# RWKV-7 scan: the second half of a triangular inverse on four 64x64 tiles of TensorE, its odd blocks swapped by VectorE transposes, with other queue orders

## The reference, cut to what matters

```python
def step(s, inp):
    r_t, w_t, k_t, v_t, a_t, b_t = inp
    sa = jnp.einsum('bhij,bhj->bhi', s, a_t)
    s = s * w_t[:, :, None, :] + sa[..., None] * b_t[:, :, None, :] + v_t[..., None] * k_t[:, :, None, :]
    return s, jnp.einsum('bhij,bhj->bhi', s, r_t)
```

## Time and profile before

| | us |
|---|---|
| median of 3 runs | 2571.04 (2567.44 to 2571.35) |
| the profiled execution, its own time | 2572.18 |
| span of the profile, first to last instruction | 2570.4 |
| stretch of the scan | 937 (1440 to 2377 us of the span) |
| one period of the scan, typical | 11.80 |
| TensorE / VectorE / ScalarE / GpSimd busy over the span | 2311.9 / 1137.1 / 798.5 / 622.8 |

### The profile page before, as it was taken

One profiled execution on the slowest core, in us unless ns is written; L12 is line 12 of the kernel. 1 busy time (PEld: TensorE's weight loads), 2 busy tenths in 40 slices (PEclk: granted clock), 3 DMA queues, 4 the chain that ended last, 5 costly groups with the idle time before them and its releaser, 6 DMA issues. The chain is left out here.

```text
span 2570.4 us, 56958 instructions
## 1 busy us (share of the span) xinstructions
PE 2311.9 (90%) x24172; PEld 1455.2 (57%) x24172; DVE 1137.1 (44%) x2231; ACT 798.5 (31%) x2003; POOL 622.8 (24%) x913
## 2 busy tenths in 40 slices
PE   5799999989969998999999598989898998988598
PEld 2355555544534443554444477777777777777354
DVE  3111111111354667002131466666666666666684
ACT  2100111102323553221000244444444444444221
POOL 0000000001221332000000444444445454544242
PEclk8899999999979998999999799999999999999699
DMA  6500000033011665555431334333333333231532
GB/s 257 212 25 16 16 16 16 16 149 129 27 41 30 176 192 157 161 154 175 163 114 58 104 92 149 92 85 94 84 94 83 92 83 93 83 95 50 186 122 87
DMA packets 296657, 261.79 MB, mean 102 GB/s; under 512 B 105440, under 2 KB 255200, under 8 KB 293856
## 3 DMA queue, kind: packets, MB, share of 16 engines
q1 hardware_dynamic: 296416, 258.32, 32.2%
HBM read 178.54 MB, written 79.69 MB: 100 GB/s over the span
## 5 line engine op out<-in xcount | busy, mean ns | idle before, releaser
L770 PE MATMUL ps<-xt,w_slab 128*128 128x512 f32 (+1 forms) x1376 | 552.7, 558 | 30.3 <-DMA w_slab<-in_w 19.5
L770 PEld LDWEIGHTS ps<-xt,w_slab 128*128 128x128 f32 x1376 | 260.1, 192 | 317.8 <-issue 259.7
L341 PE MATMUL ps<-h,fw_slab 128*128 128x512 f32 (+1 forms) x768 | 279.1, 525 | 11.4 <-DMA time_tab_ctx<-in_tctx 11.4
L1675 PE MATMUL ps<-M,AT 64*64 64x64 f32 x6400 | 270.0, 224 | 5.3 <-DVE M L1575 2.5
L1438 POOL TENSOR_TENSOR SP<-Q,decay 64x128 f32<-64x128 f32 x304 | 138.6, 456 | 462.5 <-DVE Q L1615 433.3
L1675 PEld LDWEIGHTS ps<-M,AT 64*64 64x64 f32 x6400 | 219.3, 135 | 48.7 <-issue 14.6
L1675 PE MATMUL ps<-TT,MT 64*64 64x64 f32 x5120 | 216.4, 223 | 17.8 <-ACT XT L1500 15.1
L341 PEld LDWEIGHTS ps<-h,fw_slab 128*128 128x128 f32 x768 | 146.9, 191 | 142.4 <-issue 135.8
L1675 PEld LDWEIGHTS ps<-TT,MT 64*64 64x64 f32 x5120 | 177.6, 135 | 48.8 <-issue 37.9
L1561 DVE COPY_PREDICATED TT<-mask,ps 128x256 f32<-128x256 int32 x400 | 166.8, 435 | 75.4 <-PE ps L1675 72.7
L532 POOL TENSOR_TENSOR xt<-scaled_out,xt 128x1024 f32<-128x1024 f32 x10 | 23.5, 2346 | 699.9 <-DVE scaled_out L565 699.9
(11 more groups left out here) (194 smaller groups left out, 3115.0 us busy)
## 6 DMA issues: line engine op xcount, KB each, us to landing
feat<-feature_scratch SPq DMA_DIRECT2D x160, 256.0 KB, 2.8
feature_scratch<-k_feats SPq DMA_DIRECT2D x64, 320.0 KB, 5.2
w_slab<-in_rwin SPq DMA_DIRECT2D x32, 512.0 KB, 5.9
feature_scratch<-k_feats SPq DMA_DIRECT2D x24, 640.0 KB, 6.7
mod_slab<-in_modw SPq DMA_DIRECT2D x8, 1536.0 KB, 6.6
Q<-v_token_scratch SPq DMA_DIRECT2D x320, 32.0 KB, 2.5
Z<-v_token_scratch SPq DMA_DIRECT2D x320, 32.0 KB, 2.2
fgo<-in_modw SPq DMA_DIRECT2D x8, 1024.0 KB, 10.7
```

The source lines that it names most:

```text
L341: mm = pe.matmul(ps[:, b0 + b, 0:n], wi[:, half, k, :], h0[:, k, a:a + n], start=k == 0, stop=k == KT - 1)
L770: mm = pe.matmul(ps[:, bank, 0:n], w[:, i % 2, k, :], src[:, k, a:a + n], start=k == 0, stop=k == KT - 1)
L1675: mm = pe.matmul(out[o, b, :], L[o, b, :], R[o, b, :], start=True, stop=True)
```

## The change

The second half of the inverse is laid out anew. The function `quad` takes the place of `level` for `m4` to `mt32`: still eight 64x64 matmuls, but for `t8`, `t16`, `t32`, `m8`, `m16` and `mt32` the two sub-chunks `b` of one head use different quarters of the array (rows of one partition half, output to the same or to the other half), so that four quarters are used in place of two. `m4` keeps to two quarters. The results of `b = 0` and `b = 1` go to different banks, 4 and 5; the first levels move from bank 4 to bank 3, which `products` also writes. Blocks of the odd sub-chunk lie in the other partition half between `t` and `m`, so that `MT` must have them there too: `second_mt` becomes three instructions, a transpose of 128 partitions by 128 elements and two of 64 partitions by 128 elements whose output is in the other partition half. Each of mt4, mt8 and mt16 does this.

From the moved bank follow new waits: `t2` waits for ScalarE's `BKt` copy and VectorE's `first_r` of its own chunk, and `products` 1 waits for VectorE's `t4` copy of the chunk before.

The queue orders change. VectorE: cum, mt4, t8, Q of sub-chunk 0, ak, mt8, x, t16, first_r, t2, Q of sub-chunk 1, mt16, t32, mt2, t4. TensorE: r, products 0, m4, sa, t8, products 1, state, y_state, y, m8, r, t16, sa, m16, t2, state, y_state, y, t32, m2, mt32, t4. ScalarE: R, m4, Z, exps, AT, y, m8, BKt, R, Z, m16, y, m2, XT. SyncE and GpSimd keep theirs, and no transfer is added or moved.

```diff
-DB = {"mt4": 1, "t8": 2, "mt8": 3, "t16": 4, "mt16": 5, "t32": 6}
+DB = {"mt4": 3, "t8": 4, "mt8": 7, "t16": 8, "mt16": 11, "t32": 12}
...
-    lev = lambda bank: ps[:, bank, 0:256].rearrange("p (b t) -> p b t", b=B4)
+    lev_a = ps[:, 3, 0:256].rearrange("p (b t) -> p b t", b=B4)
+    lev_b = ps[:, 4:6, 0:128]
+    two_by = lambda t: flat(t).rearrange("p (b x) -> p b x", b=2)
+    by_b = lambda t: t.rearrange("p (b d) t -> p d b t", b=2)
...
             def first_at(j, cc):
...
                 for h in two:
-                    act.activation(d4(AT[par(cc)][own(h)]), gcol(own(h), slice(2 * h, 2 * h + 2), 3 * h), ACT.Copy).then_inc(aa, 1)
+                    act.activation(by_b(AT[par(cc)][own(h)]), gcol(own(h), slice(2 * h, 2 * h + 2), 3 * h), ACT.Copy).then_inc(aa, 1)
...
             def second(j, cc, name):
                 act.wait_ge(pb, count("second", j, cc, PB["mt32" if name == "xt" else name]))
-                act.activation((XT if name == "xt" else M)[par(cc)][:], lev(5), ACT.Copy).then_inc(ab, 1)
+                if name == "xt":
+                    act.activation(XT[par(cc)][:].rearrange("p (d b) t -> p b d t", b=2), lev_b.rearrange("p b (d t) -> p b d t", d=2), ACT.Copy).then_inc(ab, 1)
+                    return
+                m = M[par(cc)]
+                act.activation(two_by(m[:, 0:4]), lev_b, ACT.Copy).then_inc(ab, 1)
...
             def period(j, c, ahead):
...
+                if Q_:
+                    r(j, c, 0)
                 if B_:
...
                 if Q_:
-                    r(j, c, 0)
+                    sa(j, c, 0)
                 if ahead or c + 3 < NCH:
                     exps(j, c + 3)
-                if Q_:
-                    sa(j, c, 0)
                 if A_:
                     first_at(j, c + 2)
+                if Q_ and is_lat(c):
+                    y(j, c, 0)
                 if B_:
...
                     first_bk(j, c + 2)
-                if Q_ and is_lat(c):
-                    y(j, c, 0)
                 if Q_:
...
             def second_t(j, cc, k):
                 v.wait_ge(pb, count("second", j, cc, PB[f"t{k}"]))
-                masked(flat(TT[k][par(cc)][:]), ps[:, 5, 0:256], 1 + LEVELS.index(k)).then_inc(db, 1)
+                v.copy_predicated(two_by(TT[k][par(cc)][:]), mask[:, 1 + LEVELS.index(k), :].rearrange("p (b x) -> p b x", b=2), lev_b).then_inc(db, 1)
...
             def second_mt(j, cc, k):
                 v.wait_ge(ab, count("act_second", j, cc, AB[f"m{k}"]))
-                v.transpose(flat(MT[par(cc)][:]), flat(M[par(cc)][:])).then_inc(db, 1)
+                m, mt = M[par(cc)], MT[par(cc)]
+                v.transpose(flat(mt[:, 0:2]), flat(m[:, 2:4])).then_inc(db, 1)
+                for h in two:
+                    v.transpose(flat(mt[other(h), 2:4]), flat(m[own(h), 0:2])).then_inc(db, 1)
...
             def state(j, c, sub):
...
                     second_t(j, c + 1, 8)
+                if Q_:
+                    state(j, c, 0)
                 if A_:
                     first_ak(j, c + 2)
-                if Q_:
-                    state(j, c, 0)
                 if B_:
...
                     second_t(j, c + 1, 16)
+                if A_ and is_lat(c + 2):
+                    first_r(j, c + 2)
                 if A_:
                     first_t(j, c + 2, 2)
+                if Q_:
+                    state(j, c, 1)
                 if B_:
                     second_mt(j, c + 1, 16)
-                if Q_:
-                    state(j, c, 1)
-                if A_:
-                    if is_lat(c + 2):
-                        first_r(j, c + 2)
-                    first_mt2(j, c + 2)
-                if B_:
                     second_t(j, c + 1, 32)
                 if A_:
+                    first_mt2(j, c + 2)
                     first_t(j, c + 2, 4)
...
                     ge(pe, drm, count("rmask", j, cc, 0))
+                else:
+                    ge(pe, da, count("dve_first", j, cc - 1, DA["t4"]))
...
-            def level(out, L, R, done):
+            def level(L, R):
...
-                        mm = pe.matmul(out[o, b, :], L[o, b, :], R[o, b, :], start=True, stop=True)
-                mm.then_inc(done, 1)
+                        mm = pe.matmul(lev_a[o, b, :], L[o, b, :], R[o, b, :], start=True, stop=True)
+                mm.then_inc(pa, 1)
...
+            def quad(rows, L, lb, R, rb, out, bank):
...
+                for d in range(NDIR):
+                    for h in two:
+                        for b in two:
+                            r, c = own(rows(h, b)), own(out(h, b))
+                            mm = pe.matmul(ps[c, bank(b), d * CK:d * CK + CK], L[r, lb(b) + d, :], R[r, rb(b) + d, :], start=True, stop=True)
+                mm.then_inc(pb, 1)
...
+            stay, cross = lambda h, b: h, lambda h, b: h ^ b
+            odd_last, odd_first = lambda b: 2 * b, lambda b: 2 - 2 * b
...
             def t2(j, cc):
...
                 pe.wait_ge(da, count("dve_first", j, cc, DA["m1"]))
+                pe.wait_ge(aa, count("act_first", j, cc, AA["bk"]))
+                if is_lat(cc):
+                    pe.wait_ge(drm, count("rmask", j, cc, 1))
                 ge(pe, da, count("dve_first", j, cc - 1, DA["t4"]))
-                level(lev(4), AT[s], M[s], pa)
+                level(AT[s], M[s])
...
             def m2(j, cc):
...
                 pe.wait_ge(da, count("dve_first", j, cc, DA["t2"]))
-                level(lev(4), MT1[s], TT[2][s], pa)
+                level(MT1[s], TT[2][s])
...
             def t4(j, cc):
...
                 pe.wait_ge(aa, count("act_first", j, cc, AA["m2"]))
-                level(lev(4), AT[s], M[s], pa)
+                level(AT[s], M[s])
...
             def m4(j, cc):
...
                 ge(pe, ab, count("act_second", j, cc - 1, AB["xt"]))
-                level(lev(5), MT[s], TT[4][s], pb)
+                quad(stay, MT[s], odd_last, TT[4][s], odd_last, stay, lambda b: 5 - b)
...
             def t(j, cc, k):
...
                 pe.wait_ge(ab, count("act_second", j, cc, AB[f"m{k // 2}"]))
-                level(lev(5), AT[s], M[s], pb)
+                quad(stay, AT[s], odd_last, M[s], odd_first, cross, lambda b: 4 + b)
...
             def m(j, cc, k):
...
                 pe.wait_ge(db, count("dve_second", j, cc, DB[f"t{k}"]))
-                level(lev(5), MT[s], TT[k][s], pb)
+                quad(cross, MT[s], odd_last, TT[k][s], odd_last, stay, lambda b: 5 - b)
...
             def mt32(j, cc):
...
                 pe.wait_ge(db, count("dve_second", j, cc, DB["t32"]))
-                level(lev(5), TT[32][s], MT[s], pb)
+                quad(cross, TT[32][s], odd_last, MT[s], odd_last, stay, lambda b: 4 + b)
...
             def state(j, c, sub):
                 l = lng(c)
-                if not is_lat(c):
-                    pe.wait_ge(asa, count("four", j, c, 2 * sub + 2))
+                pe.wait_ge(asa, count("four", j, c, 2 * sub + 2))
...
             def y_state(j, c, sub):
                 l = lng(c)
-                pe.wait_ge(asa, count("four", j, c, 2 * sub + 2))
                 if sub == 0:
...
                     r(j, c, 0)
-                if B_:
-                    m4(j, b)
                 if A_:
...
                 if B_:
-                    t(j, b, 8)
+                    m4(j, b)
                 if Q_:
                     sa(j, c, 0)
+                if B_:
+                    t(j, b, 8)
                 if A_:
                     products(j, a, 1)
-                if B_:
-                    m(j, b, 8)
-                if lat:
-                    y_state(j, c, 0)
                 if Q_:
...
                 if lat:
+                    y_state(j, c, 0)
                     y(j, c, 0)
+                if B_:
+                    m(j, b, 8)
                 if Q_:
...
                     sa(j, c, 1)
+                if B_:
+                    m(j, b, 16)
                 if A_:
                     t2(j, a)
-                if B_:
-                    m(j, b, 16)
-                if lat:
-                    y_state(j, c, 1)
                 if Q_:
...
                 if lat:
+                    y_state(j, c, 1)
                     y(j, c, 1)
+                if B_:
+                    t(j, b, 32)
                 if A_:
...
                 if B_:
-                    t(j, b, 32)
+                    mt32(j, b)
                 if A_:
                     t4(j, a)
-                if B_:
-                    mt32(j, b)
...
-    smask = np.stack([np.repeat(m, 2, axis=1).reshape(P, 256) for m in tab_levels], axis=1)
+    smask = np.stack([np.tile(m, (1, 2, 1)).reshape(P, 256) for m in tab_levels], axis=1)
...
```

More of the change, by code:

```diff
@@ L1267 @@
 DA = {"ak0": 1, "ak1": 2, "mt1": 3, "m1": 4, "t2": 5, "mt2": 6, "t4": 7}
-DB = {"mt4": 1, "t8": 2, "mt8": 3, "t16": 4, "mt16": 5, "t32": 6}
+DB = {"mt4": 3, "t8": 4, "mt8": 7, "t16": 8, "mt16": 11, "t32": 12}
 LAT_ONLY = lambda n: [0, 0] + [n] * (NCH - 2)
```

(25 more changed lines are left out.)

## The result

The changed kernel takes 2769.52 us (median of four runs, 2768.79 to 2771.19) against 2571.19 before: ratio 1.0775, 95% interval 1.0757 to 1.0794. It is slower by 198 us. The forecast was 2651, +80, with a range from 2566 to 2700: the direction is right, the size is not, and the time lies outside the range.

The account below looks back on a forecast made before the run. No engine is full; a period is one chain through all engines. It grows from 11.80 to 12.77 us (12.1 with context), +10.0 per column tile, +80 over eight: 2651 us, range 2566 to 2700.

Parts of the forecast that it names:

- The granted clock is 1.00: Scan windows of the kernel before: clock read as 1.00 (2.4 GHz) in all three; the new chain has no clock term.
- sa at 6.6 and `m16` at 8.0: TensorE in the new period, us after `r`: both listed as work beside VectorE's chain and covered by it.
- The hand-over from RBK to `t2`: VectorE to TensorE: `t2` now waits for RBK; 0.05 us allowed, as for other hand-overs between engines.
- triple transposes: VectorE's mt4, mt8, mt16: three transposes of 0.31 each, 0.91 us in place of 0.37; bounds 0.64 and 1.33.
- the x pair: VectorE's x work between mt8 and the t16 mask: 0.91 us on the chain, read from the earlier trace.
- Q to ak: VectorE, Q of sub-chunk 0 to the start of ak behind it: 0.64 us on the chain.
- The chain of the period: Scan, from `r` to `r` through all engines: 12.77 us against 11.80; 12.1 in the two context periods of ten.
- Four quarters: TensorE levels on four quarters: full gain taken, 0.45 us from start to end against 0.68, 0.28 to the same shape.
- A: The forecast: VectorE's chain longer by two triple transposes and ak; 2651 us, own range 2608 to 2718, chance 0.63.
- B: VectorE chain as in A, but four quarters no faster than two: `t8` and `mt32` +0.23 each, 2688 us; chance 0.15.
- C: No change: the transposes hide and TensorE's `t32` and `m2` hold the period at about 11.7; 2565 to 2572, chance 0.08.
- D: Faster: earlier Q reaches the next `r`, 10.8 a period, 2489 us; needs under 3.5 us from Q to `t2`; chance 0.14.

Follow-up runs that it names:

- the filler kernel: Changed kernel plus 24 idle 64x64 matmuls on TensorE between the second sa and m16 of every period; 2685.35 us, ratio 1.0458.
- the split alone: Kernel before with each of mt4, mt8 and mt16 cut into three transposes, nothing swapped, levels on two quarters; 2653.40 us, ratio 1.0326.
- the orders alone: Kernel before with the changed kernel's VectorE, ScalarE and TensorE queue orders, one transpose each, levels on two quarters; 2614.62 us, ratio 1.0175.
- the one-transpose kernel: Changed kernel with one 128x256 transpose for the three of mt4, mt8 and mt16, four quarters kept, inverse not the reference's; 2670.77 us, ratio 1.0393.

## Why the prediction was wrong, point by point

**The step that failed: "The granted clock is 1.00".** The forecast read it from the earlier trace rows and carried it over to the new period without asking what the change does to it: a term of the sum put at nothing. It also wrote down a rest of TensorE and took it as cover: sa at 6.6 and `m16` at 8.0 leave about 0.95 us (8.0 less 6.6 and 0.45). Measured are 1.56. Filled with idle matmuls, that rest gives 84 us back (2769.5 to 2685.4) at a clock of 1.00. That is most of the 118 us between 2651 and 2769.

**The terms that were too small.** GpSimd's collision with the x mask, which the forecast does not have, is 20 of the 34 us between 2651 and 2685 (moved away: 2665.1). The hand-over from RBK to `t2` was 0.05 in the sum and 0.26 in the filler kernel's trace; with one wait left out it is 0.14, and 9 us are gone (2656.3). What remains is 5, and it is the rest of terms of both signs. In a latent period of the filler kernel two triple transposes take 0.10 more than the 0.91 of the sum each, the hand-over 0.21 more, and the x pair 0.37 more (1.28, 1777.00 to 1778.28, for 0.91); Q to ak takes 0.12 less (0.52 for 0.64). The rule read from the earlier trace rows, that a VectorE instruction of 128 partitions overlaps the next by 0.08 and one of 64 leaves 0.03, does not hold: the 128-partition transpose at 2087.94 leaves 0.03, and Q on 64 partitions overlaps ak by 0.08.

**The terms that held.** The chain of the period: 12.77 and 12.1 worked out, 12.84 and 12.06 at the full clock. For 12.84 that is in part luck. The triples and the late `t2` are in that period too, and are paid back by Q to ak (0.52 for 0.64), ak to mt8 (0.80 for 0.90) and an x mask that GpSimd did not hold (0.45). A latent period at the full clock, which the 12.77 was meant for, is 13.48. Four quarters: 0.45 from first start to last end, 0.46 measured. The price of one transpose: 0.31, as measured.

**Two sums.** The total is added up as it says, but the list of what the change adds (1.0 earlier, 0.90, twice 0.54, 0.28) comes to +1.2 a period and not to the +0.97 beside it; the total goes by the chain, not by the list. And the column tile of before, added up the same way, would be 8 x 11.80 + 2 x 11.40 = 117.2, not 116.39, so that some 6 of the 80 us come from the method.

**The rivals.** A was the right chain with the clock missing and the prices above too small. B (four quarters run no faster) is refuted by the 0.46. The rule of the Trainium skill that stood beside it ("TensorEngine Tiling (Array Packing)", section "Restrictions and Gotchas"), on row tiles and one bank, has no stall to show here either: the two partition halves still share a bank in every level. The traces do not agree with the page there. C (the transposes hide) is refuted by the split alone. D (the earlier Q carries through) is refuted by the orders alone: Q came at 4.4 where it had been at 5.2, and the period grew from 11.80 to 12.55. Its break-even, 3.5 us of work between Q and `t2`, was not reached: the changed kernel has 5.05 (2086.42 to 2091.47).

**What stays open.** Why a stall and a denser packing of matmuls add up in the clock as they do is not settled: the runs order the cases (0.85, 0.88, 0.91, 0.99, 1.00) but do not separate what is counted. The time with work in flight does not separate them: full-clock periods of the split kernel (10.82 of 12.87 us) and of the one-transpose kernel (10.44 of 12.37) have nearly the same share, and the clocks of the kernels are 0.99 and 0.88. A half dose of fillers, or the long stall in the kernel before, was not tried.

## What to carry to other kernels

A change that makes TensorE's work shorter, while something else sets the period, buys idle time, and idle time can cost the clock, as here: in a sum for such a change the clock is a term, to be priced by the rows of a longer stall, not a constant. Before adding a layout trick, walk the chain once through all engines and look for an instruction that waits in its queue behind others whose results are needed later; here that was worth 67 us with two moved calls. And when VectorE work is shifted in time, look at what GpSimd does then, for instructions with two SBUF inputs.

## What the runs showed of the hardware

Four groups of 64x64 matmuls on four quarters run side by side: eight matmuls, sixteen records, 0.46 us from first start to last end against 0.68 on two. A fall of the granted clock to 1.2 GHz followed a rest of TensorE of 1.56 us after a stretch of ordinary work. In the first period of the scan, with the same orders and rests of 0.94 (ahead of `m16`) and 1.42 (ahead of `mt32`), the clock stayed at 1.00. The Trainium skill, "TensorE: Matmul & The Clock Gate", section "What's actually happening", says that the clock depends on how busy the engine has been lately; the traces agree, since matmuls that nobody reads bring it back. VectorE transposes: 128 elements take 0.31 on 128 partitions. On 64 they take 0.31 where the output lies in the other partition half and 0.28 where it does not (means of the changed and of the split kernel), and the instruction ahead is not overlapped in the first case; three together take 1.02 and 0.86 to the next start. A VectorE mask with both inputs in SBUF takes 0.45 alone and 0.87 beside GpSimd's `bk`.
